# Gating tables built once for all 128 columns, with half of each kept in DRAM scratch until the output products

## The reference

```
q  = (xc @ wq).reshape(PEER_CHUNK, PEER_HEADS, 2, half)
sc = einsum('chpd,hpnd->chpn', q, sub_keys)
s1, i1 = top_k(sc[:, :, 0], 16);  s2, i2 = top_k(sc[:, :, 1], 16)
cand = (s1[..., :, None] + s2[..., None, :]);  cidx = i1[..., :, None] * 128 + i2[..., None, :]
top_s, pos = top_k(cand, 16);  eidx = take_along_axis(cidx, pos)
g = softmax(top_s)
a = gelu(einsum('chkd,cd->chk', u[eidx], xc))
return einsum('chk,chkd->cd', g * a, v[eidx])
```

## Time and profile before

| | before |
|---|---|
| median of 3 runs | 2781.81 us (2775.86 to 2782.1) |
| profiled execution | 2776.63 us |
| its span | 2774.8 us |
| TensorE busy | 2634.4 us, 95% |
| VectorE busy | 1833.4 us, 66% |
| ScalarE busy | 1202.4 us, 43% |
| DMA, mean | 140 GB/s |

### The profile page before, as it was taken

The page is one execution under the profiler, slowest core; times in us unless marked ns, Lnnn a source line. Parts: engine busy times, 40 slices in busy tenths (PEclk is TensorE's granted clock), DMA queues, the critical chain, the costliest instruction groups (busy, mean ns, idle before and its releaser), DMA issues.

```text
span 2774.8 us, 46869 instructions
## 1 busy us (share of the span) xinstructions
PE 2634.4 (95%) x18927; PEld 2355.6 (85%) x18927; DVE 1833.4 (66%) x3513; ACT 1202.4 (43%) x2501; POOL 555.0 (20%) x415
## 2 busy tenths in 40 slices
PE   8899999998997999999999999899799999999997
PEld 7779788996787999999888877679799999888886
DVE  4757144447669846777887556759965777888656
ACT  5432135444443454334444555344354333444554
POOL 3500134555075500000000002247420000000000
PEclk9999799999898999999999999899899999999999
DMA  5300045565043554444444555124455444444554
GB/s 183 113 1 9 27 149 167 183 186 156 6 147 116 188 182 154 145 145 144 145 149 149 196 193 167 46 99 150 141 182 168 145 145 145 145 152 145 182 191 151
DMA packets 109174, 387.58 MB, mean 140 GB/s; under 512 B 11808, under 2 KB 12192, under 8 KB 108576
## 3 DMA queue, kind: packets, MB, share of 16 engines
q1 hardware_dynamic: 105168, 371.77, 40.9%
q0 software_dynamic: 2192, 8.86, 0.9%
q10 hardware_dynamic: 1600, 3.96, 0.4%
HBM read 383.49 MB, written 1.05 MB: 139 GB/s over the span
## 4 chain that ended last, share of the span: by engine, by line
PE 81%; DVE 14%; ACT 2%; DMA 1%; issue 1%; POOL 1%; DVEq 0%; ACTq 0%; SPq 0%
PE pb L414 80%; PE pb L423 2%; DVE arena L2020 1%; DVE arena L2012 1%; DVE arena L2014 1%; DVE arena L2009 1%; DVE arena L2017 1%; DVE arena L1841 1%; DVE arena L1414 1%; DVE arena L1411 1%; ACT arena L1025 1%; DVE arena L2043 1%; DVE arena L1561 1%; POOL lo L2180 0%; DVE H L1788 0%
## 5 line engine op out<-in xcount | busy, mean ns | idle before, releaser
L1013 ACT CAST hi<-raw 128x512 fp32r<-128x512 f32 x1402 | 824.1, 620 | 504.1 <-PE pb L414 443.5
L414 PE MATMUL pb<-HTh,hi 128*128 128x256 f32 (+1 forms) x2968 | 863.0, 291 | 35.5 <-DVE lo L1428 27.9
L414 PE MATMUL pb<-HTl,hi 128*128 128x256 f32 (+1 forms) x2968 | 847.0, 285 | 0.0
L414 PE MATMUL pb<-HTh,lo 128*128 128x256 f32 (+1 forms) x2968 | 846.2, 285 | 0.0
L2180 POOL TENSOR_TENSOR lo<-raw,hi 128x512 fp32r<-128x512 f32 x387 | 538.1, 1409 | 694.4 <-ACT hi L1013 694.1
L414 PEld LDWEIGHTS pb<-HTh,hi 128*128 128x128 f32 x2968 | 577.9, 195 | 38.7 <-DVE lo L1428 28.3
L1421 DVE TENSOR_TENSOR lo<-raw,hi 128x1024 fp32r<-128x1024 f32 x432 | 527.1, 1221 | 112.1 <-ACT hi L1013 112.1
L414 PEld LDWEIGHTS pb<-HTl,hi 128*128 128x128 f32 x2968 | 575.7, 194 | 0.9
L414 PEld LDWEIGHTS pb<-HTh,lo 128*128 128x128 f32 x2968 | 574.8, 194 | 0.0
L414 PE MATMUL pb<-hi,WH 128*128 128x512 f32 x1112 | 446.7, 402 | 6.9 <-DVE WL L2143 6.9
L414 PE MATMUL pb<-hi,WL 128*128 128x512 f32 x1112 | 435.1, 391 | 0.0
(11 more groups left out here) (192 smaller groups left out, 2407.0 us busy)
## 6 DMA issues: line engine op xcount, KB each, us to landing
raw<-in_uT SPq DMA_DIRECT2D x256, 512.0 KB, 3.2
raw<-in_vT SPq DMA_DIRECT2D x256, 512.0 KB, 3.2
raw<-in_w_ffn_in SPq DMA_DIRECT2D x44, 512.0 KB, 3.8
raw<-in_wq SPq DMA_DIRECT2D x32, 512.0 KB, 3.3
raw<-in_w_in SPq DMA_DIRECT2D x24, 512.0 KB, 3.8
raw<-in_w_ffn_out SPq DMA_DIRECT2D x22, 512.0 KB, 4.4
raw<-in_w_gate SPq DMA_DIRECT2D x16, 512.0 KB, 3.6
raw<-in_w_o SPq DMA_DIRECT2D x16, 512.0 KB, 3.2
```

Source lines behind the costliest of these rows:

```text
L414: return e.matmul(o, l, r, start=start, stop=stop)
L1013: e.copy(u.hi[k], u.half[k]).then_inc(*s.up("hi", ("hi", g)))
```

## The change

Each table is now built once, for all 128 columns: O2 and GO are twice as wide, there is one buffer of each instead of two (O1 and GO), and TensorE's 12 matmuls have 128 columns and fill a whole bank. This happens in u steps 64 to 127. VectorE multiplies the first 64 columns from PSUM as before. ScalarE copies the other 64 (`keep`) to one of two SBUF buffers, and SP stores them to DRAM scratch (128 KB each). In v steps 0 to 63 no table is built; SP brings table q back behind the load of unit v(q+4), into one of four buffers, and `gated(q, 64)` reads it from there and waits for it. Some constants (cos and sin beside negd) now lend their space too and are fetched again for layer 1.

```diff
         def g_mm(q, j0):
@@ tensor @@
-                    x = mm(PB[b][:, k * 64:(k + 1) * 64], m.O1[q % 2][:, :, k], m.GO[q % 2][:, p, :, k], p == 0, p == 2)
+                    x = mm(PB[b][:, k * 128:(k + 1) * 128], m.O1[:, :, k], m.GO[:, p, :, k], p == 0, p == 2)
...
         for j in range(128):
-            if j < 64:
-                g_mm(j, 64)
@@ scalar @@
+        def keep(q):
+            w.wait_ge(*s.to("g_ps", l, q))
+            if q > 1:
+                w.wait_ge(*s.to("stored", l, q - 2))
+            src = PB[q % 4][:, :].rearrange("p (t j) -> p t j", t=4)[:, :, 64:128]
+            e.copy(m.GS1[q % 2].rearrange("p (t j) -> p t j", t=4), src).then_inc(*s.up("kept", ("kept", l, q)))
+
         def u_step(j):
             take("u", l, j)
+            if j >= 64:
+                keep(j - 64)
@@ vector @@
-            tt(m.O2, m.IOT[:, j0:j0 + 64, :], i2, ALU.is_equal).then_inc(*up("onehots", ("o2", l, j0, q)))
+            tt(m.O2, m.IOT, i2, ALU.is_equal).then_inc(*up("onehots", ("o2", l, q)))
+            if q:
+                w.wait_ge(*s.to("g_ps", l, q - 1))
...
+            x = tt(m.GO, m.O2.unsqueeze(1).to_broadcast([128, 3, 128, 4]),
+                   m.GP[:, :, t4].unsqueeze(2).to_broadcast([128, 3, 128, 4]), M)
...
         def gated(q, j0):
+            if j0:
+                gv = m.GL[q % 4].rearrange("p (t j) -> p j t", t=4)
+                w.wait_ge(*s.to("returned", l, q))
+            else:
+                gv = PB[q % 4][:, :].rearrange("p (t j) -> p j t", t=4)[:, 0:64, :]
+                w.wait_ge(*s.to("kept", l, q))
+            tt(av, av, gv, M).then_inc(*s.up("gated", ("gated", l, j0, q)))
...
         for j in range(128):
-            if j < 63:
-                onehots(j + 1, 64)
@@ sync @@
+    def store(l, q):
+        w.wait_ge(*s.to("kept", l, q))
+        e.dma_start(m.kept[l, q], m.GS1[q % 2]).then_inc(*s.up(f"stored{q % 2}", ("stored", l, q), by=16))
+
+    def bring(l, q):
+        w.wait_ge(*s.to("stored", l, q))
+        w.wait_ge(*(s.to("gated", l, 64, q - 4) if q > 3 else s.to("g_ps", l, 63)))
+        e.dma_start(m.GL[q % 4], m.kept[l, q]).then_inc(*s.up(f"returned{q % 4}", ("returned", l, q), by=16))
...
         e.dma_start(u.slot, u.src).then_inc(*s.up(u.slot_key, ("raw", i), by=16))
+        if u.name[0] in ("u", "v") and len(u.name) == 3:
+            l = u.name[1]
+            n = u.name[2] + (128 if u.name[0] == "v" else 0)
+            if 68 <= n < 132:
+                store(l, n - 68)
+            if 132 <= n < 196:
+                bring(l, n - 132)
```

More of the change, by code:

```diff
@@ L230, with __init__ @@
 class Memory:
-    def __init__(self, T, PB, d, out):
-        self.T, self.PB, self.d = T, PB, d
+    def __init__(self, T, PB, d, out, kept):
+        self.T, self.PB, self.d, self.kept = T, PB, d, kept
         self.raw, self.hi, self.lo = T["raw"], T["hi"], T["lo"]
@@ L339, in __init__ @@
         self.AW = arena[:, :].rearrange("p (j t) -> p j t", j=128)
-        lent = self.C("negd")
-        self.IT = [wk[:, 0:128].bitcast(BF), lent[:, 0:128].bitcast(BF), wk[:, 1664:1920]]
+        o = CONST["cos"][0]
+        self.lent, self.lent_src = self.cst[:, o:o + 768], d["consts"][:, o:o + 768]
+        self.IT = [wk[:, 0:128].bitcast(BF), self.lent[:, 0:128].bitcast(BF), wk[:, 1024:1280]]
         self.GP = wk[:, 128:512].bitcast(BF).rearrange("p (w t) -> p w t", w=3)
         self.IOT = wk[:, 512:768].bitcast(BF).rearrange("p (n k) -> p n k", k=4)
-        self.O1 = [wk[:, o:o + 256].bitcast(BF).rearrange("p (n k) -> p n k", k=4) for o in (768, 1024)]
-        self.O2 = lent[:, 128:256].bitcast(BF).rearrange("p (n k) -> p n k", k=4)
-        self.GO = [wk[:, o:o + 384].bitcast(BF).rearrange("p (w n k) -> p w n k", w=3, k=4) for o in (1280, 1664)]
+        self.O1 = wk[:, 768:1024].bitcast(BF).rearrange("p (n k) -> p n k", k=4)
+        self.O2 = self.lent[:, 128:384].bitcast(BF).rearrange("p (n k) -> p n k", k=4)
+        self.GO = wk[:, 1024:1792].bitcast(BF).rearrange("p (w n k) -> p w n k", w=3, k=4)
+        self.GS1 = [wk[:, 1792:2048], self.lent[:, 384:640]]
+        self.GL = [wk[:, 768 + i * 256:1024 + i * 256] for i in range(4)]
         self.BC2 = self.AW[:, 96:104, :].rearrange("p j t -> p (j t)")
@@ L951, in u_step, with g_mm @@
             free[b] = [("act", l, j)]
-        def g_mm(q, j0):
+        def g_mm(q):
             b = q % 4
             emptied(b)
-            w.wait_ge(*s.to("go", l, j0, q))
+            w.wait_ge(*s.to("go", l, q))
             for k in range(4):
                 for p in range(3):
-                    x = mm(PB[b][:, k * 64:(k + 1) * 64], m.O1[q % 2][:, :, k], m.GO[q % 2][:, p, :, k], p == 0, p == 2)
-            x.then_inc(*s.up("peer_ps", ("g_ps", l, j0, q)))
-            free[b] = [("gated", l, j0, q)]
+                    x = mm(PB[b][:, k * 128:(k + 1) * 128], m.O1[:, :, k], m.GO[:, p, :, k], p == 0, p == 2)
+            x.then_inc(*s.up("peer_ps", ("g_ps", l, q)))
+            free[b] = [("gated", l, 0, q)]
         for j in range(64):
@@ L973, in tensor @@
         for q in range(64):
-            g_mm(q, 0)
+            g_mm(q)
             u_step(64 + q)
         for j in range(128):
-            if j < 64:
-                g_mm(j, 64)
             u = units.take("v", l, j)
@@ L1865, in vector @@
         o = 136 * l
+        if l:
+            w.wait_ge(*s.to("lent"))
         for g in range(4):
@@ L1903, in at_scores @@
             if g:
-                if l:
-                    w.wait_ge(*s.to("negd"))
                 stt(m.WS[i], C("negd"), 8.0 * 2.0 ** -(hh + 1), src, M, A).then_inc(*up("scores"))
@@ L2091, in gate_parts, with onehots @@
                 x.then_inc(*up("places", *([("gate_parts", l)] if p else [])))
-        def onehots(q, j0):
+        def onehots(q):
             t4 = slice(4 * q, 4 * q + 4)
-            i1 = m.IT[0][:, t4].unsqueeze(1).to_broadcast([128, 128, 4])
-            i2 = m.IT[1][:, t4].unsqueeze(1).to_broadcast([128, 64, 4])
-            own()
-            tt(m.O2, m.IOT[:, j0:j0 + 64, :], i2, ALU.is_equal).then_inc(*up("onehots", ("o2", l, j0, q)))
[L2100 to L2108, removed]
+            own()
+            i2 = m.IT[1][:, t4].unsqueeze(1).to_broadcast([128, 128, 4])
+            tt(m.O2, m.IOT, i2, ALU.is_equal).then_inc(*up("onehots", ("o2", l, q)))
+            if q:
+                w.wait_ge(*s.to("g_ps", l, q - 1))
+            i1 = m.IT[0][:, t4].unsqueeze(1).to_broadcast([128, 128, 4])
+            tt(m.O1, m.IOT, i1, ALU.is_equal).then_inc(*up("onehots"))
+            w.wait_ge(*s.to("o2", l, q))
+            x = tt(m.GO, m.O2.unsqueeze(1).to_broadcast([128, 3, 128, 4]),
+                   m.GP[:, :, t4].unsqueeze(2).to_broadcast([128, 3, 128, 4]), M)
+            x.then_inc(*up("onehots", ("go", l, q)))
         def gated(q, j0):
@@ L2112, in gated @@
             w.wait_ge(*s.to("act", l, j0 + 63))
-            w.wait_ge(*s.to("g_ps", l, j0, q))
-            tt(av, av, PB[q % 4][:, 0:256].rearrange("p (t j) -> p j t", t=4), M).then_inc(*s.up("gated", ("gated", l, j0, q)))
+            if j0:
[5 more added lines that the diff above has]
+            tt(av, av, gv, M).then_inc(*s.up("gated", ("gated", l, j0, q)))
         for j in range(64):
@@ L2130, in vector @@
                 gate_parts()
-                onehots(0, 0)
+                onehots(0)
         for q in range(64):
             if q < 63:
-                onehots(q + 1, 0)
-            else:
-                onehots(0, 64)
+                onehots(q + 1)
             gated(q, 0)
@@ L2147, in vector @@
         for j in range(128):
-            if j < 63:
-                onehots(j + 1, 64)
-            elif j == 63:
+            if j == 63:
                 gated(63, 64)
@@ L2241, in gpsimd @@
                 if l == 0:
-                    o = CONST["negd"][0]
-                    e.dma_start(m.C("negd"), d["consts"][:, o:o + 512]).then_inc(*s.up("negd_in", ("negd",), by=16))
+                    e.dma_start(m.lent, m.lent_src).then_inc(*s.up("lent_in", ("lent",), by=16))
     w.wait_ge(*s.to("bc", 4))
@@ L2280, in program @@
         PB = [ctx.enter_context(nc.psum_tensor(f"pb{i}", [128, 512], F32)) for i in range(8)]
-        m = Memory(T, PB, d, out)
+        kept = nc.dram_tensor("kept", (2, 64, 128, 256), F32).ap()
+        m = Memory(T, PB, d, out, kept)
         s = Signals()
```

## The result

| | before | after |
|---|---|---|
| median | 2778.84 us (4 runs, 2774.33 to 2782.1) | 3145.78 us (4 runs, 3143.68 to 3152.69) |
| profiled execution, its span | 2776.63, 2774.8 us | 3143.68, 3141.9 us |
| TensorE busy | 95% | 87% |
| mean granted clock | 0.967 | 0.939 |

Ratio 1.1326, 95% interval 1.1299 to 1.1353: the change makes the kernel 367 us slower. The forecast of 3009 us had the direction and the place, but the time lies outside its range (2930 to 3110).

What follows compares the result with a forecast made beforehand. TensorE, busy 95% of the span, was taken to bound the kernel. The profiled 2776.6 us plus 12 (wider gating matmuls) plus 218 (waits for returned tables) gave 3006.6; 3009 us was named, range 2930 to 3110.

Steps and rivals of the forecast that it cites:

- closed round: V steps 0 to 63: each table return hangs on the previous split; 5.27 us a step instead of 3.57, +218 us.
- Part 2: V steps 0 to 63: second building of tables goes away, 3.57 to 2.71 us a step, at most 110 us less.
- L: V steps 0 to 63: time from issue of the load to landing of the returned table, taken as 3.65 us.
- multiply to split: V steps 0 to 63, VectorE: from the start of the multiply to the split's start, 0.33 us.
- split, issue: V steps 0 to 63: the split takes 1.22 us, and SP issues the load 0.02 us after it ends.
- the matmul term of Part 1: U steps 64 to 127: 12 gating matmuls of 128 columns at 66 ns, +0.09 us a step, +12 us.
- The estimate of +34 us: U steps 64 to 127: gating matmuls at the skill's 81 ns instead of 59, 0.26 us a step; left beside the sum.
- VectorE and ScalarE in the u steps, and the stores: U steps 64 to 127: wider product, added PSUM copy and 128 KB stores fit beside TensorE's work and cost nothing.
- return overtakes the load: V steps 0 to 63: return lands near 2.33 us, round 3.95 us, kernel 2838 us; chance 0.07.
- The return is hidden: V steps 0 to 63: return lands in 1.1 us, round 2.71 us, kernel 2679 us; chance 0.03.
- VectorE also binds in the u steps: U steps: slow product or single buffer adds 38 us, kernel 3045 us; chance 0.08, shared with slower loads.
- The clock: V steps 0 to 63: TensorE at half clock needs 5.28 us a step, no more than the round, so nothing charged.

Runs made afterwards that it cites:

- two one-operand experiments: The changed kernel with one gating matmul operand read as 128 neighbouring elements: moving operand 3055.1 us, weights 3143.9 us.
- the kernel before with pairs: The kernel before, with GO stored as pairs of tokens, written by two VectorE instructions of 384 elements: 2703.2 us, ratio 0.9718.

## Why the prediction was wrong

The mechanism was right: the closed round of split, load, return, multiply and split sets the v steps, TensorE idles in it, and the whole gain of Part 2 is gone behind it. The failure is one of size: three terms were too small, and nothing offset them. Term by term, for 128 steps:

| term | forecast | measured | missed |
|---|---|---|---|
| gating matmuls, per u step | +0.09 us | 4.30 - 3.66 = +0.64 | 70 us |
| L and waking up, issue of the load to the multiply | 3.65 + 0.05 | 5.82 - 0.02 - 0.53 - 1.22 = 4.05 | 45 us |
| multiply to split | 0.33 | 0.53 | 26 us |
| split, issue | 1.24 | 1.24 | 0 |

The multiply row is the mean from its start to that of the split. Forecast +12 and +218; measured 128 x 0.64 = 82 and 128 x (5.82 - 3.57) = 288, together 370, beside 367 us between the spans. (The sum of 3006.6 and the 5 us up to the median would be 3012, not 3009; that changes nothing here.)

1. *The step that failed is the matmul term of Part 1*, "128 columns should take 53 + 13 = 66 ns". It took the price of a column from float32 operands that lie in a row and put it on bf16 columns with a gap of 8 bytes. The rows had the contradiction in them: by that formula 64 columns should have taken 27 + 13 = 40 ns, and they took 59. I explained the 19 ns by the weight load, and set the upper bound (86 ns) by the same idea. The two one-operand experiments show that the weight load had next to no part in it (108 ns with the weights in a row, 56 with the moving operand). The estimate of +34 us from the 81 ns of the Trainium skill, "TensorE: Matmul & The Clock Gate", section "Back-to-back issue gap", was nearer, and too low too.
2. *L*: the queueing was right; the return lands 0.44 us behind the load on average (median 0.32), and I took 0.45. What was off is the load, 3.6 us for 3.2, though its size and queue are the same. Shown, not explained.
3. *The multiply*: I took the time of the read from PSUM for one from SBUF with the same jumps. No bound was drawn for this term.
4. *VectorE and ScalarE in the u steps, and the stores*: cost nothing, as forecast. The product took 951 ns (forecast 950).
5. *The rivals*: "return overtakes the load" is out: in after none of the 128 returns that stand right behind a load landed before it (0.29 us behind at the least). "The return is hidden" needed a landing in 1.1 us; with the return asked for two splits sooner it is hidden at 3.5 us and more, and the kernel is then indeed faster than before. "VectorE also binds in the u steps" is out too: the u steps are 4.30 us, but VectorE waits in them for TensorE.
6. *The clock*: in after part of some v steps ran at 1.2 GHz (granted clock 0.50, 0.43 us from one 512-column matmul to the next, below) and the rest at 0.23 us, and the chain, of which TensorE is no part there, shows no cost of it.

```profile
1427.20:1430.00 2.80, 2.80 (x8) 2.23 (x7) 0.00 (x0) 0.18 (x1) 0.00 (x0) 0.50 0.63 228
...
1427.59 0.63 PE L417 MATMUL pb<-hi,WH 128*128 128x512 f32 x1
1428.01 0.63 PE L417 MATMUL pb<-lo,WH 128*128 128x512 f32 x1
```

## What to carry to other kernels

A prefetch that is issued from a program in order comes no sooner than the wait ahead of it: follow what the wait hangs on, and if the consumer of the prefetch stands ahead of it, the latency is paid in every step, however many buffers there are. Where a short instruction takes longer than its formula, settle why before scaling it; here the unexplained 19 ns was the largest error, and, once explained, worth 73 us in the kernel before. Look at the step in bytes of both operands on every engine: a layout that is fast for the writer can halve the reader.

## What the runs showed of the hardware

- TensorE reads a bf16 moving operand at half rate when elements are 8 bytes apart (0.81 ns a column, 59 ns for 64, 111 for 128), and at about full rate when they are 4 or 2 bytes apart (58 and 56 ns for 128). A gap of 8 bytes in the weights cost next to nothing (111 ns with it, 108 without; 3143.7 and 3143.9 us). The Trainium skill, "SBUF — State Buffer", section "Door 1: The DMA port swizzle", says that two accesses per 16-byte line are enough for full bandwidth, so that 8 bytes would be free; for TensorE's moving operand the measurement says otherwise, and decides.
- In the v steps with gating products the first matmul behind them takes 0.31 to 0.32 us where the others take 0.23 (before, and the kernel before with pairs).
- VectorE: a float32 read from SBUF with a step of 256 bytes makes 256 elements 0.615 us instead of 0.425. A product with runs of two bf16 elements keeps the fast form (550 ns for 768). With columns side by side it leaves it (950 for 768, 1748 for 1536); there one operand repeats one number per run and the other is read with a step of 8 bytes, and which of the two does it was not tested.
- A 128 KB DMA behind a 512 KB one on SP's queue lands 3.5 us after its issue (median), ahead of it 2.0 us.
